# Writing the gates of 64 of 384 tokens into DRAM by GpSimd scatter-add instead of by one-hot matmul products

## The reference

```python
def peer_ffn(xn, w_query, sub_keys, expert_u, expert_v):
    ...
        q = (xb @ w_query).reshape(c, PEER_HEADS, 2, HALF_QUERY)
        s = jnp.einsum('chpd,pkd->chpk', q, sub_keys)
        s_top, i_top = lax.top_k(s, PEER_TOPK)
        ...
        best, pos = lax.top_k(cand.reshape(c, PEER_HEADS, PEER_TOPK * PEER_TOPK), PEER_TOPK)
        idx = jnp.take_along_axis(cand_idx.reshape(c, PEER_HEADS, PEER_TOPK * PEER_TOPK), pos, axis=-1)
        g = jax.nn.softmax(best.astype(jnp.float32), axis=-1).astype(xb.dtype)
        u = jnp.take(expert_u, idx, axis=0)
        act = jax.nn.gelu(jnp.einsum('chkd,cd->chk', u, xb), approximate=False)
        vsel = jnp.take(expert_v, idx, axis=0)
        return jnp.einsum('chk,chkd->cd', g * act, vsel)
```

## Time and profile before

| | us |
|---|---|
| median of 3 runs (lowest to highest) | 3430.11 (3427.84 to 3430.18) |
| the profiled execution's own time | 3430.59 |
| its span | 3428.4 |
| PE busy | 3372.4 (98%) |
| DVE busy | 2636.6 (77%) |
| ACT busy | 1240.9 (36%) |
| POOL busy | 807.9 (24%) |
| mean DMA rate | 219 GB/s |

### The profile page before, as it was taken

The page is one execution under the profiler, slowest core; times in us unless marked ns, Lnnn a source line. Parts: engine busy times, 40 slices in busy tenths (PEclk is TensorE's granted clock), DMA queues, the critical chain, the costliest instruction groups (busy, mean ns, idle before and its releaser), DMA issues.

```text
span 3428.4 us, 47304 instructions
## 1 busy us (share of the span) xinstructions
PE 3372.4 (98%) x16086; PEld 2750.7 (80%) x16086; DVE 2636.6 (77%) x5503; ACT 1240.9 (36%) x1980; POOL 807.9 (24%) x661
## 2 busy tenths in 40 slices
PE   8999999999999999999999999999999999999998
PEld 4458855898899898888854688559988888998887
DVE  4673389997888888888736734999978888888887
ACT  2332223794322323333214332339833333322332
POOL 0000026002333333333300000440033333333332
PEclk9999999999999999999999999999999999999999
DMA  4313303468888888888741132145698888888885
GB/s 123 105 37 92 129 27 126 171 247 318 319 304 303 305 302 308 305 308 309 260 158 37 38 115 89 44 141 193 240 354 308 306 309 308 302 304 306 303 303 204
DMA packets 270646, 750.58 MB, mean 219 GB/s; under 512 B 19741, under 2 KB 139293, under 8 KB 243904
## 3 DMA queue, kind: packets, MB, share of 16 engines
q1 hardware_dynamic: 196768, 480.57, 39.9%
q0 software_dynamic: 73760, 268.47, 22.8%
HBM read 681.86 MB, written 67.11 MB: 218 GB/s over the span
## 4 chain that ended last, share of the span: by engine, by line
PE 80%; DVE 14%; DMA 3%; POOL 1%; ACT 1%; issue 1%; SPq 0%; DVEq 0%; ACTq 0%; POOLq 0%
PE ps L1239 29%; PE ps L1225 22%; PE ps L1029 7%; PE ps L898 4%; PE ps L1122 4%; DVE OHS L2143 3%; PE ps L1087 3%; PE ps L876 2%; DVE OHS L2139 2%; PE ps L1205 2%; PE ps L1176 2%; DMA ROWS<-v_rows_dram,GIS 1%; DVE URAWL L2109 1%; PE ps L1008 1%; PE ps L843 1%
## 5 line engine op out<-in xcount | busy, mean ns | idle before, releaser
L778 POOL DMA_INDIRECT ROWS<-v_rows_dram,GIS x256 | 330.6, 1291 | 578.7 <-DVE X L2213 486.5
L778 POOL DMA_INDIRECT ROWS<-u_rows_dram,GIS x256 | 300.4, 1174 | 610.4 <-DVE STG L2197 543.6
L1578 ACT ACTIVATE AC<-ps 128x384 f32<-128x384 f32 x192 | 94.5, 492 | 926.4 <-PE ps L1225 926.4
L1239 PE MATMUL ps<-VHI,WHI 128*128 128x512 f32 x1536 | 414.9, 392 | 4.7 <-DVE WLO L2178 4.2
L1239 PE MATMUL ps<-VLO,WHI 128*128 128x512 f32 x1536 | 415.2, 392 | 0.0
L1239 PE MATMUL ps<-VHI,WLO 128*128 128x512 f32 x1536 | 411.3, 390 | 0.0
L1571 ACT CAST VHI<-VRAW 128x512 fp32r<-128x512 f32 x512 | 285.8, 619 | 326.9 <-PE ps L1239 323.1
L2213 DVE SCALAR_TENSOR_TENSOR X<-ROWS,STG,X 128x1024 f32<-128x1024 f32 x256 | 328.4, 1283 | 23.1 <-DMA ROWS<-v_rows_dram,GIS 11.0
L1239 PEld LDWEIGHTS ps<-VLO,WHI 128*128 128x128 f32 x1536 | 288.8, 188 | 63.7
L1239 PEld LDWEIGHTS ps<-VHI,WLO 128*128 128x128 f32 x1536 | 288.6, 188 | 62.2
L1239 PEld LDWEIGHTS ps<-VHI,WHI 128*128 128x128 f32 x1536 | 285.6, 188 | 53.9 <-DVE WLO L2178 5.3
(11 more groups left out here) (281 smaller groups left out, 5344.9 us busy)
## 6 DMA issues: line engine op xcount, KB each, us to landing
VRAW<-v_dram SPq DMA_DIRECT2D x128, 1024.0 KB
URAW<-ut_dram SPq DMA_DIRECT2D x128, 512.0 KB, 3.7
URAW<-ut_dram SPq DMA_DIRECT2D x64, 1024.0 KB, 5.9
g_table<-GST SPq DMA_DIRECT2D x12, 4096.0 KB, 12.9
GT<-g_table SPq DMA_DIRECT2D x62, 768.0 KB, 8.3
WR<-w_in_dram SPq DMA_DIRECT2D x8, 2048.0 KB, 12.0
WR<-w_in_dram SPq DMA_DIRECT2D x32, 512.0 KB, 4.7
WR<-w_q_dram SPq DMA_DIRECT2D x8, 2048.0 KB, 8.0
```

Of the source, the lines that this page charges most:

```text
L778: pool.indirect_dma_start(out=ROWS[:, k % GR, :], out_offset=None, in_=table, in_offset=bass.IndirectOffsetOnAxis(ap=GIS[:, par, k:k + 1], ...
L1239: last = nc.tensor.matmul(ps[:, 2 + o, :], a[:, par, jj, b * P:(b + 1) * P], c[:, dh, jj, :], start=(first and n == 0), stop=(final and n ...
```

## The change

Per layer, the table chunk of the first 64 tokens is no longer made by products. Instead:

- SP fills that chunk of `g_table` (4 MB) with zeros, early in stage D, from a small zeroed tile `ZERO` that POOL sets.
- DVE computes for each pick of the first 128 tokens the number of its 4-byte cell in the table (`table_cells`, four small instructions, once for heads 0 to 5 after group 3 of 4, once for heads 6 and 7 at the end of D). SP moves, by two DMAs each time (`move_cells`), half of the picks of tokens 0 to 63 onto partitions 64 to 127, so that one transfer carries two picks of each of the 64 tokens.
- POOL issues 64 indirect DMAs with an add, 128 elements of 4 bytes each, into the cells. Before each head it waits until all transfers of the heads before have landed, so that no cell is added to by two transfers at once.
- Stage E has 40 slots, in five chunks of 64 tokens (`CHUNKS`). The 136 pieces of early work are spread over 40 slots. The staged picks `IDS` and `NEGG` have two buffers of 64 tokens instead of one of 128.
- `store_gates` stands in SP's program after the last slot of its chunk. After `load_pair(1, 1)` SP waits for all 64 scatters (`scattered`) and loads the first 64 tokens' gates of step 0 (`first_gates(0, 1)`, 128 KB), ahead of `load_v(0, 1)` and `load_one(1, 1)`. `weigh_early` of step 0 waits for it.
- Three semaphores became one (`dot_steps`), another pair one as well, and one small DVE instruction at the program's start makes the partition numbers `PART`.

The core of the diff:

```diff
-TOK_IT = 128
+CHUNKS = DT // CB - 1
+ZERO_RUN = 512
+HALF_PICKS = TOPK // 2
...
-    E_SLOTS, E_CHUNKS = DT // OH, KC * (NG - TAIL_EARLY - 1)
+    E_SLOTS, E_CHUNKS = CHUNKS * CB // OH, KC * (NG - TAIL_EARLY - 1)
...
                     weights([(at_cols(0, KC, 512), cols_of(l, w_q, 512 * i, 512))])
+                    if i == 2:
+                        sp.wait_ge(pool_zeros, 3)
+                        sp.dma_start(gd[0].rearrange("i j c -> i (j c)").rearrange("i (r n) -> i r n", n=ZERO_RUN),
+                                     ZERO[:].unsqueeze(1).to_broadcast([P, NK * CB // ZERO_RUN, ZERO_RUN])
+                                     ).then_inc(zero_stored, 16)
...
+                def first_gates(b0, b1):
+                    sp.dma_start(GT0[:, b0:b1].rearrange("p b j c -> p b (j c)"),
+                                 gd[b0:b1, :, 0:JG, :].rearrange("b i j c -> i b (j c)")).then_inc(g_loaded[0], 16)
+
+                def move_cells(done, h0, h1):
+                    sp.wait_ge(sel_ready, done)
+                    for t in (SCI, SCW):
+                        halves = t.rearrange("p (h s m) -> p h s m", s=2, m=HALF_PICKS)
+                        sp.dma_start(halves[CB:P, h0:h1, 0, :], halves[0:CB, h0:h1, 1, :]).then_inc(cells_moved, 16)
...
+                    if e == CELLS_AT:
+                        move_cells(CELLS_A, 0, PH - HG)
+                move_cells(CELLS_B, PH - HG, PH)
+                sp.wait_ge(zero_stored, 16)
+                for q in range(E_SLOTS):
+                    if (q + 1) % (CB // OH) == 0:
+                        u = q // (CB // OH)
+                        store_gates(u)
+                        if u == CHUNKS - 2:
+                            for past in range(u):
+                                sp.wait_ge(g_stored[gate_half(past)], 16 * (past // 2) + 32)
+                            first_gates(1, CHUNKS - 1)
+                            for g in range(2):
+                                sp.wait_ge(es_stored[g], 16)
+                                load_pre(g, g)
+                    for c in early_chunks(q):
+                        if c % KC == KC - 1:
+                            pass_early(TAIL_EARLY + c // KC)
+                pass_early(NG - 1)
                 load_pair(1, 1)
+                sp.wait_ge(scattered, 16 * TOPK // 2 * PH * (l + 1))
+                first_gates(0, 1)
                 load_v(0, 1)
                 load_one(1, 1)
...
+                pool.wait_ge(zero_stored, 16)
+                for h in range(PH):
+                    pool.wait_ge(cells_moved, 32 if h < PH - HG else 64)
+                    if l or h:
+                        pool.wait_ge(scattered, 16 * HALF_PICKS * (PH * l + h))
+                    for k in range(TOPK * h, TOPK * h + HALF_PICKS):
+                        pool.indirect_dma_start(out=cells, out_offset=bass.IndirectOffsetOnAxis(ap=SCI[:, k:k + 1], axis=0),
+                                                in_=SCW[:, k:k + 1], in_offset=None, compute_op=ALU.add
+                                                ).then_inc(scattered, 16)
...
+                def table_cells(count, h0, h1):
+
+                    part = slice(TOPK * h0, TOPK * h1)
+                    first, second, weight = (SEL[:, k, 0, h0:h1].rearrange("p h m -> p (h m)") for k in range(3))
+                    dve.wait_ge(sel_ready, count - 1)
+                    nc.vector.tensor_copy(SCW[:, part], weight)
+                    st.did(nc.vector.scalar_tensor_tensor(GIF[:, part], first, float(NK), second, ALU.mult, ALU.add))
+                    st.then(dve)
+                    st.did(nc.vector.tensor_scalar(GIF[:, part], GIF[:, part], float(CB), PART, ALU.mult, ALU.add))
+                    st.then(dve)
+                    nc.vector.tensor_copy(SCI[:, part], GIF[:, part]).then_inc(sel_ready, 1)
...
                     if i >= 1:
                         finish_group(i - 1)
+                    if i == NGRP - 1:
+                        table_cells(CELLS_A, 0, PH - HG)
...
                 finish_group(NGRP - 1)
+                table_cells(CELLS_B, PH - HG, PH)
...
                     dve.wait_ge(pre_loaded[par], use * 16)
-                    dve.wait_ge(g_loaded[par], use * 16)
+                    dve.wait_ge(g_loaded[par], use * 16 + 16 * (1 - par))
```

More of the change, by code:

```diff
@@ L324, in encoder @@
     WF1, _ = sb("WF1", [P, DT])
-    NEGG, _ = sb("NEGG", [P, TOK_IT])
+    SCI, _ = sb("SCI", [P, PICKS], I32, offset=preb_at + 8 * DT)
+    SCW, _ = sb("SCW", [P, PICKS], offset=preb_at + 8 * DT + 4 * PICKS)
+    ZERO, _ = sb("ZERO", [P, ZERO_RUN], offset=preb_at)
+    assert 2 * PICKS <= DT and ZERO_RUN <= 2 * DT and end_d <= preb_at
+    NEGG, _ = sb("NEGG", [P, 2, CB])
     end_f = at[0]
@@ L350, in encoder @@
     GMX, GSUM = SMALL[:, 44:52], SMALL[:, 52:60]
+    PART = SMALL[:, 60:61]
+    cells = gd.rearrange("b i j c -> (b i j c)").unsqueeze(1)
     first_loads, pos_loaded = sem("first_loads"), sem("pos_loaded")
@@ L364, in encoder @@
     rows_loaded = [sem(f"rows_loaded{i}") for i in range(GR)]
+    scattered = sem("scattered")
     ROWS_LAYER = 16 * 2 * PICKS // GR
@@ L404, in encoder @@
     oh_act = lsem("oh_act")
+    zero_stored, cells_moved = lsem("zero_stored"), lsem("cells_moved")
     before_late = len(layer_sems)
@@ L450, in g_all_stored, with gate_half @@
         for s in halves:
-            e.wait_ge(g_stored[s], 16 * (DT // TOK_IT) + 16)
+            e.wait_ge(g_stored[s], 16 * len(range((s + 1) % 2, CHUNKS, 2)) + 16)
+    def gate_half(u):
+        return (u + 1) % 2
     def early_slot(e):
@@ L1608, in _ @@
                     step(it, 1)
-                act.wait_ge(dots_done, GSTEPS)
-                nc.scalar.activation(DOT[:], DOT[:], ACT.Gelu).then_inc(gelu_done, 1)
+                act.wait_ge(dot_steps, GSTEPS)
+                nc.scalar.activation(DOT[:], DOT[:], ACT.Gelu).then_inc(dot_steps, 1)
                 with act.Fori(GSTEPS // 2, (NG - 2) // 2) as it:
@@ L1702, in filter_angles @@
                         sine_arguments()
+                pre.did(nc.vector.tensor_tensor_reduce(FK[:, 0:P], ident, iota, 1.0, 0.0, ALU.mult, ALU.add, accum_out=PART))
                 dve.wait_ge(dec_loaded, 64)
@@ L2142, in _ @@
                         t = q0 + c
-                        last = nc.vector.tensor_scalar(OHS[:, q % OHR, 1, c, :], iota, IDS[:, 1, t:t + 1],
-                                                       IDS[:, 2, t:t + 1], ALU.is_equal, ALU.mult)
+                        last = nc.vector.tensor_scalar(OHS[:, q % OHR, 1, c, :], iota, IDS[:, u % 2, 1, t:t + 1],
+                                                       IDS[:, u % 2, 2, t:t + 1], ALU.is_equal, ALU.mult)
                         if c in (3, OH - 2):
```

93 lines of the change are left out of this document (41 added, 52 removed).

## The result

| | before | after |
|---|---|---|
| median of 4 runs (lowest to highest), us | 3429.37 (3427.84 to 3430.18) | 3449.41 (3448.78 to 3453.36) |
| the profiled execution | 3430.59 | 3448.85 |
| its span | 3428.4 | 3447.0 |

The ratio is 1.0062, with a 95% interval of 1.005 to 1.0074. The change makes the kernel **slower by 20 us**, which is more than the 0.2% that a measurement can tell.

What follows compares the result with a forecast made beforehand. It took PE and DVE as almost equally late in stage E, beside loads on a shared queue. Per layer -2.6 (E) +1.0 (cells) +1.0 (F's start) = -0.6, twice -1.2: from 3430.59 to 3429 us, range 3403 to 3462.

Steps and rivals of the forecast that it cites:

- Step 1: Stage E: eight slots fewer, PE the longer engine at 3.56 us a slot; -16.9 us a layer, E 156.3.
- rival D: Stage E: slots already set by loads alone, so removing eight shifts nothing; 3434 us, chance 0.05.
- Step 2: Stage E: early loads queued behind stores land late, PE stalls 3.6, 0, 3.6 and 2.0; +11 us, bounds 0 and 16.
- Steps 3 and 4: Stage E: POOL's scatters delay DVE, +2.5 us (bounds 0 and 9.6); scatter traffic, +0.8 (bounds 0 and 5).
- Step 3: Stage E: scatters cost DVE's one-hot instructions 0.15 us a meeting, 5.8 us, about half showing; +2.5 us a layer.
- Step 5: Stage D: four cell-number instructions (table_cells) on DVE's full stream; +1.0 us a layer.
- Step 6: From stage D's end: scatters end between 730 and 759 us, SP asks near 789; cost 0, cover 30 to 60 us.
- Step 7: Start of F: step 0's gates come behind the 1 MB load, weighing follows them; +1.0 us, bounds -1.8 and +4.
- Step 8: Early stage D: the 4 MB of zeros, 12.9 us, go out while DMA engines are mostly idle; 0 us.
- B: Stage E: DVE loses 0.15 us at every one-hot instruction beside POOL's scatters; 3460 us, chance 0.16.
- A: Stage E: bank and buffer slack takes most load stalls, leaving 2 us; 3411 us, chance 0.26.
- C: Start of F: scatters of 3.5 us each end late and hold SP back 63 us a layer; 3555 us, chance 0.08.

Runs made afterwards that it cites:

- e3: Changed kernel with a third cast buffer for early weights and the first four gate stores each put behind the next early load; 3440.9 us.
- e1: Changed kernel with a third buffer for the cast early weights, so a cast waits for PE's e - 3 instead of e - 2; 3442.3 us.
- e2: Changed kernel with each of the first four gate stores put behind the next early load, still two cast buffers; 3433.3 us.
- e4: Changed kernel without the 64 scatters of each layer (first 64 tokens' gates left out); 3444.9 us.
- e5: e3 without the 64 scatters of each layer (first 64 tokens' gates left out); 3396.9 us.
- e6: e3 with 12 scatters of heads 0 and 1 begun earlier, in stage D; output unchanged; 3407.1 us.
- e10: e6 with each gate store cut into two halves, the second behind the early load after next (last chunk's halves together); 3399.3 us.
- e11: e10 without the early start: all 64 scatters after stage D, stores still in halves, three cast buffers; 3422.1 us.

## Why the prediction was wrong, step by step

- **Step 1, eight slots (-16.9): right.** E without stalls is 156.4 us in e3 (predicted 156.3), the slot 3.56, so rival D is refuted. (The "7 of the 173.2" that it called waits are too many: the table has PE busy for 170.6 of them. The sum doesn't use it.)
- **Step 2, late loads (+11, bounds 0 and 16): the step that failed. It measured 24.7.** The mechanism and the places were right: loads behind stores land after 12 to 13.4 us, ACT's cast waits 5 to 7 us, PE stalls before slots 12, 28 and 37. Three things were missed. *First*, a fourth stall, before slot 21, where the text has "needed late enough (no stall)". I had followed the one path from the load over cast, low part and one-hot matrices to PE, but not what is queued behind the waiting cast on ACT: the copies that free PE's banks. This path is the shorter one, and it made the stalls of slots 21 and 28. *Second*, the waits themselves: 6.1, 3.1, 4.35 and 4.3 us, 17.9 in all, instead of 3.6, 0, 3.6 and 2.0. Of the 2.5 us more at the first, 2.1 are the store, which left 5.5 us after slot 7's start and not 3.46, as the trace of before had it; the text didn't ask whether ACT would still copy in time once a cast stands ahead of these copies. *Third*, the clock: a stop of PE costs also what runs slower behind it, 6.8 us in four places, which no term had. The two cast buffers were not costed either. e1 puts them at 5.5 us of E's end while the loads are late, e3 against e2 at 2.8 when they are not.
- **Steps 3 and 4, scatters beside DVE and their traffic (+3.3): the number came out, 3.1 us in e4, by luck.** Step 3 has 5.8 us more on DVE a layer, at 0.15 us a meeting; DVE's packs of seven are 0.02 us longer, 0.9 us in 40 slots. Half of the 3.1 us is a fall of the clock that e4 doesn't have. Once nothing stalls, the scatters cost E nothing (e3 against e5).
- **Step 5, cells (+1.0):** `SEL` is ready 0.1 us later, and the first gate products come at 624.48 instead of 622.95, 1.5 later; that part lies in E.
- **Step 6, scatters in time (0, with 30 to 60 us of cover): cost 0, but the cover was wrong.** A scatter takes 2.04 us on average and 0.30 of gap instead of 1.6 in all, and once POOL stood 7.1 us in the middle of a head. The waits for landings, 30.3 us a layer, are within the 24 to 53 reckoned. The last scatter was issued at 786.4, with the end estimated between 730 and 759. SP asked at about 800 only because E was 11 us longer than forecast. One wrong step covered the other: in e3, where E ends 25 us earlier, they are 28 us late. The rule "in time until 2.5 us each" holds for 3 us a landing and SP asking at 789; in e3 seven landings take 52.4 us and SP asks at about 776.
- **Step 7, start of F (+1.0):** +0.3. **Step 8, the zeros (0):** `SEL` is no later than step 5 allows, though the 4 MB landed after 20.1 us instead of 12.9.
- The sum, layer 0: E -2.6 forecast, +8.9 measured; D and F's start +2.0 forecast, +0.4 measured.
- **Rivals.** B gives a time on the same side (3460) by a mechanism that e4 refutes as the cause: 0.9 us more of DVE's time a layer instead of 27, and all scatters together 3.1 us. That the measured time lies in the stated range is due to the range, not to the forecast's account. A (small stalls) is refuted. C was the hidden second bound, and it decides as soon as the stalls are mended.

## What to carry to other kernels

When a change makes a loop shorter, look again at every transfer and scatter that the loop's length used to cover, since the old trace shows their waits as zero up to the point where they decide. For each instruction that may come to wait, list what stands behind it on its own engine, for here that path was shorter than the path of its data. Put urgent small loads ahead of large stores on a shared queue, and after one bound is mended look for the next one that it had covered.

## What the runs showed of the hardware

- **A stop of PE of 3 to 6 us can end at half the granted clock, but need not:** in the change 16 gate products took 3.4 to 3.7 us instead of 1.95 behind stops of 5.92, 2.95, 4.18 and 4.17 us, and then the clock was whole again. In e4 they took 2.05 behind a stop of 3.64 us, at 1.00. In e3, with no such stop in E, there was no such slot.
- **A scatter-add of 128 elements of 4 bytes keeps POOL for 1.54 to 3.78 us**, 2.04 on average, longer than a gather of expert rows (1.29 on average). POOL waits 2.2 to 2.5 us for a head's landing in five of seven cases of layer 0, and 8.6 and 10.0 us in the two where the head's last scatter was issued less than 10 us behind a 4 MB store, although stores are issued by SP. The rows of the change:

```profile
622.18 2.58 POOL L810 DMA_INDIRECT g_table<-SCW,SCI  x1 [2.29 <-DMA g_table<-SCW,SCI]
...
671.59 1.54 POOL L810 DMA_INDIRECT g_table<-SCW,SCI  x1 [10.04 <-DMA g_table<-SCW,SCI]
```

  The Trainium skill ("DMA: Bandwidth & Descriptors", "Queues, rings and completion order") says that each DMA engine takes turns between its queues, packet by packet. By that alone one would expect so small a transfer to land soon; it does not explain the 10.04 us, and what holds them up was not tried by itself.
- **Halving the stores shortened the longest wait for a landing** from 13.7 us (e6) to 7.9 (e10), and from 13.6 (e3) to 12.0 (e11), in one profiled run each.
